# Experts taken in a pattern of ranks by row count, and padding rows left out of the scatter, in a decoder layer with 32 experts

## The chip, the cores and the metric

One core of a Trainium2 chip. The metric is the device time of one execution in microseconds.

## The reference

One layer of a decoder: 512 prompt rows and 8 single-row samples (520 rows of 1024 numbers) go through a combined projection, three mixers (pooling, dilated attention, convolution), an output projection and a layer norm. Then comes the part that matters here, a mixture of experts (fp32 throughout):

```python
logits = xt @ router_w + router_b                 # 520 x 32
top_v, top_i = lax.top_k(logits, 4); gates = softmax(top_v)
hh = xblk @ e_w_in[e] + e_b_in[e]                 # 1024 -> 2048
gate, up = split(hh); gate = min(gate, 7); up = clip(up, -7, 7)
act = gate * sigmoid(1.702 * gate) * (up + 1)
y = act @ e_w_out[e] + e_b_out[e]                 # 1024 -> 1024, weighted by the gate, summed per row
x = layer_norm(alpha * x + moe(x))
```

Each row goes to 4 of the 32 experts, 2080 row visits in all. The weights of one expert are 12 MiB and are used by nobody else.

## The kernel before, in words

`first_block` computes everything up to the router: projection, mixers, first layer norm (`ln1`), router (`route`), and `acc_start`, which writes alpha * x plus the gated output biases to `acc_rows` in DRAM. At its end it counts the rows of each expert. The counts come from five matmuls (L957) into `bS[0]`, and `group_table` (L1219) turns them into groups: each expert's rows are cut into groups of GS = 32, at least one per expert, in the order of the experts. VectorE works out `ends` (the last group of each expert) and, for each group, its expert, its number within the expert, and the ring position. `fields` is turned by TensorE (L964) and `group_rows` packs it into `jobs`. TensorE's bias products of the last two row tiles (`expert_bias`, L924 and L928) stand between the count and that turn. `first_block` ends as a block, and `moe_block` begins on all engines after it.

`moe_block` takes one group after the other. A group is spread over four column groups of the TensorE array, 32 rows in each: `up` multiplies the 32 gathered rows with the eight 1 MiB units of `e_in` (L1473 adds the bias, L1480 multiplies), VectorE and ScalarE make the activation, `down` multiplies with the four 1 MiB units of `e_out` (L1492), ScalarE scales with the gate (L1559). TensorE runs up of group g, then down of group g - 1, then the small matmuls that find the rows of group g + 3 (L1463). GpSimd gathers a group's rows from `x1_rows` (L1412, 128 pieces of 1 KB, with a bounds check that leaves out pads) and adds the result to `acc_rows` by an accumulating indirect DMA (L1419, 128 pieces of 1 KB). A group with fewer than 32 rows is filled with pads; their pieces are added to 32 extra rows of `acc_rows`, from PAD0 on, which are zeroed beforehand.

The weights come through a ring of NSLOT = 18 slots of 1 MiB, so one and a half experts. SyncE issues them in order, expert by expert (L214 by `load`): units 0 to 5 of an expert go into slots that the expert before the last has left (seen by its last group), units 6 to 11 into slots of the expert before it:

```python
was = (j - (NSLOT - UNITS)) % UNITS
if end is not None and was < KT:
    sp.wait_ge(up_done, KT * end + 1 + was)
elif end is not None:
    sp.wait_ge(down_done, NQ * end + 1 + was - KT)
load_unit(sp, unit(slot), e, j, slot)
```

Here `end` is the number of the last group of the expert that used the slot. The loops over groups have room for 96 (MAXG), and groups beyond the last pass as empty turns. When the last scatter has landed, `acc_rows` is read back and the second layer norm makes the output.

Of the kernel before, what the change touches and what calls it, by code (L numbers as in the profile page):

```python
# [29 lines left out]
P = 128  # L30
# [34 lines left out]
NROW = R + GS  # L65


def _columns(widths):
# [10 lines left out]
    ("over", MAXR), ("group", 1), ("third", 10), ("id32", GS)])  # L79
# [22 lines left out]
def constants():  # L102
# [32 lines left out]
    put("third", np.tile(3 * np.arange(1, 11), (P, 1)))  # L135
    put("id32", (p[:, None] % GS == np.arange(GS)) & (p[:, None] < 3 * NE))
# [44 lines left out]
def layer(nc, xT, x_prompt, x_sample, pool_prefix, conv_prefix, state_pool, state_conv, cache_k, cache_v,  # L181
          w_in, pool_w, chan, w_o, ln1_g, ln1_b, router_w, router_b, e_in, e_brow, e_out, e_bout,
          ln2_g, ln2_b, consts, ranks, pbias,
          y_prompt, y_sample, p_pool, p_conv, p_k, p_v, s_pool, s_conv, s_k, s_v):
    x1_dram = nc.dram_tensor("x1_rows", [R, D], F32).ap()
    acc_dram = nc.dram_tensor("acc_rows", [NROW, D], F32).ap()

    with ExitStack() as outer:
        def keep(name, shape, dt=F32):
            return outer.enter_context(nc.sbuf_tensor(name, shape, dt))  # L190

        def sem(name):
            return outer.enter_context(nc.semaphore(name))


        ring = keep("ring", [P, UNITS, 2048])
        cst = keep("cst", [P, NCONST])
        slot_rank = keep("slot_rank", [P, GS * (MAXR + 2)], F16)
        rankm = keep("rankm", [P, NT + 1, NE])
        gates = keep("gates", [P, NT + 1, NE])  # L200
        brow = keep("brow", [P, NQ, 2, QC], BF16)
        jobs = keep("jobs", [1, 3, NGT], I32)
        ends = keep("ends", [1, NE], I32)

        def C(name, rows=P):
            lo, hi = CONST[name]
            return cst[0:rows, lo:hi]

        unit_in = [sem(f"unit_in{u}") for u in range(NSLOT)]

        def load_unit(eng, room, e, j, slot):

            src = e_in[bass.ds(e, 1), j] if j < KT else e_out[bass.ds(e, 1), j - KT]
            eng.dma_start(room, src.rearrange("o p n -> p (o n)")).then_inc(unit_in[slot], 16)  # L214

        first_block(nc, locals())
        moe_block(nc, locals())
# [3 lines left out]
def first_block(nc, o):  # L221
# [3 lines left out]
    ring, rankm, gates, jobs, ends, brow, C, load_unit = (  # L225
        o[k] for k in "ring rankm gates jobs ends brow C load_unit".split())
# [29 lines left out]
    with ExitStack() as ctx:  # L256
# [37 lines left out]
        ssc = sb("ssc", [P, 2, NH * NS])  # L294
# [6 lines left out]
        jf = late[0:1, 2 * D + 14 * NE:2 * D + 14 * NE + 3 * P].rearrange("p (k g) -> p k g", k=3)  # L301
        btok = xtok[:, :, :].rearrange("p u n -> p (u n)")
# [20 lines left out]
        zero = cpre[:, 0:2].rearrange("p i b t -> p (i b t)")[:, 0:D // 4]  # L323
# [19 lines left out]
        zero_made = bsem("zero_made")  # L343
# [31 lines left out]
        pads_zeroed = bsem("pads_zeroed")  # L375
# [15 lines left out]
        brow_ready = bsem("brow_ready")  # L391
        fields_ready = bsem("fields_ready")
# [103 lines left out]
        def _(gp):  # L496
# [50 lines left out]
            nc.gpsimd.memset(zero, 0.0).then_inc(zero_made, 1)  # L547
# [9 lines left out]
        def _(a):  # L557
# [95 lines left out]
            def ln1_root(i):  # L653
# [5 lines left out]
            a.wait_ge(zero_made, 1)  # L659
            a.dma_start(acc_dram[PAD0:PAD0 + GS, :].rearrange("r (c n) -> (r c) n", n=QC), zero  # L660
                        ).then_inc(pads_zeroed, 16)
# [38 lines left out]
            a.wait_ge(pads_zeroed, 16)  # L700
# [4 lines left out]
        def _(pe):  # L705
# [250 lines left out]
            for j in range(NT + 1):  # L956
                mm = nc.tensor.matmul(bS[0][:, (NT + 1) * NE:(NT + 2) * NE], trib[0:rows(j), 1], memb[0:rows(j), j],  # L957
                                      start=j == 0, stop=j == NT)
            mm.then_inc(rank_done, 1)
            for i in (NT - 1, NT):  # L960
                expert_bias(i)
# [7 lines left out]
        def _(d):  # L969
# [249 lines left out]
            def group_table():  # L1219

                COUNT, SUM, SUM2, PASSED, BASE = range(5)
                row = lambda k: tab[:, k]
                ch.do(V.tensor_copy(row(COUNT), bS[0][:, (NT + 1) * NE:(NT + 2) * NE]))
# [14 lines left out]
                ch.do(V.tensor_scalar(fields[:, 1:2], fields[:, 3:4], float(NE - 1), None, ALU.min))  # L1238
                ch.mark(V.tensor_tensor(fields[:, 5:6], C("group"), fields[:, 4:5], ALU.subtract))
                ch.do(V.tensor_scalar(thirds, C("third"), fields[:, 1:2], None, ALU.is_le))  # L1240
                ch.mark(V.tensor_reduce(fields[:, 6:7], thirds, AX.X, ALU.add))
                ch.do(V.tensor_scalar(fields[:, 2:3], fields[:, 5:6], float(MAXR), None, ALU.min))
                V.tensor_tensor(fields[:, 0:1], fields[:, 1:2], fields[:, 6:7], ALU.add).then_inc(fields_ready, 1)
# [33 lines left out]
def moe_block(nc, o):  # L1277

    ring, slot_rank, rankm, gates, brow, jobs, ends, C, sem, load_unit, unit_in = (
        o[k] for k in "ring slot_rank rankm gates brow jobs ends C sem load_unit unit_in".split())  # L1280
# [4 lines left out]
    with ExitStack() as ctx:  # L1285
# [83 lines left out]
        def _(sp):  # L1369
            def end_of(e):  # L1370
                return sp.value_load(ends[0:1, bass.ds(e, 1)], min_val=0, max_val=MAXG - 1)
# [11 lines left out]
            ahead = NSLOT - UNITS  # L1383
            for j in range(ahead):
                load(1, 1, j, None)
            end0 = end_of(0)
            for j in range(ahead, UNITS):
                load(1, 1, j, end0)
            sp.dma_start(l2g[:, :], o["ln2_g"].partition_broadcast(P)).then_inc(ln2_in, 16)
            sp.dma_start(l2b[:, :], o["ln2_b"].partition_broadcast(P)).then_inc(ln2_in, 16)  # L1390
            with sp.Fori(0, (NE - 2) // 3) as three:
                for i in range(3):
                    before, last_but_one = end_of(3 * three + i + 1), end_of(3 * three + i)
                    for j in range(UNITS):
                        load(3 * three + i + 2, (i + 2) % 3, j, last_but_one if j < ahead else before)
# [10 lines left out]
        def _(gp):  # L1406
# [10 lines left out]
            def scatter(c, i):  # L1417
# [3 lines left out]
                    in_=y[:, i], in_offset=None, compute_op=ALU.add).then_inc(scattered, 16)  # L1421
# [344 lines left out]
```

## Time and profile before

| | |
|---|---|
| median of three runs | 1549.1 us (1548.63, 1549.1, 1553.25) |
| the profiled execution | 1553.53 us |
| its span | 1551.6 us |
| mean granted TensorE clock | 0.906 |
| groups, experts | 82, 32 |
| first block | to about 386 us |
| groups, first start to last start | 398.3 to 1487.3 us |
| HBM read | 446.7 MB |

A profile row of the form "L1480 PE MATMUL pu<-ring,xgT" is a group of instructions of one line of the kernel on one engine. A timeline row gives the start in us, the length in us, and after "idle before" how long the engine had been idle and what ended that. The expert part is 70% of the span, so it's read group by group: each group's first matmul has the line L1473.

### The profile page before, as it was taken

The page shows a single profiled execution, that of the slowest core. Times are in us where ns is not written, and L with a number is a line of the kernel's source. Part 1 is how long each engine was busy: PE and PEld are TensorE (multiplying, and loading weights), DVE is VectorE, ACT ScalarE, POOL GpSimd, SP SyncE. Part 2 cuts the span into 40 slices and gives each one's busy share as a digit, 9 for nine tenths or more (in the row PEclk, how much of TensorE's full clock was granted, in tenths as well). Part 3 has the DMA queues.
Part 4 walks back from the last instruction along what each step waited for, and adds up shares of the span by engine and source line. Part 5 has one row for each costly group of instructions (what it writes and reads, how often), then busy time and mean ns, then how long its engine had stood idle before and what let it go on. Part 6 is the DMA issues. An engine that isn't in the chain of part 4 may idle for free.

```text
span 1551.6 us, 35703 instructions
## 1 busy us (share of the span) xinstructions
PE 1305.5 (84%) x12455; PEld 582.6 (38%) x12456; DVE 539.4 (35%) x1798; ACT 151.4 (10%) x330; POOL 298.1 (19%) x247
## 2 busy tenths in 40 slices
PE   5998889997687978999976888999889999989960
PEld 5885333563232323333321332333323333333420
DVE  1994522236331322333321332333223333323325
ACT  0003232021000000000000000000000000000002
POOL 7000231100120211222220221222112222222223
PEclk9999679876797989999986998999999999999985
DMA  9600432116799899999899999949999779999553
GB/s 307 185 3 31 161 97 109 45 55 263 315 408 416 314 416 412 403 368 407 334 412 421 418 412 413 410 150 410 414 414 377 296 259 371 407 412 414 200 175 114
DMA packets 93495, 463.47 MB, mean 299 GB/s; under 512 B 10676, under 2 KB 37265, under 8 KB 43693
## 3 DMA queue, kind: packets, MB, share of 16 engines
q1 hardware_dynamic: 74315, 432.95, 68.8%
q0 software_dynamic: 16640, 22.30, 6.7%
q10 hardware_dynamic: 2514, 7.88, 1.3%
q8 instruction: 15, 0.25, 0.1%
q14 instruction: 11, 0.09, 0.0%
HBM read 446.66 MB, written 19.42 MB: 300 GB/s over the span
## 4 chain that ended last, share of the span: by engine, by line
PE 52%; DMA 15%; issue 5%; DVE 1%; SPq 0%; POOLq 0%; POOL 0%; ACT 0%; ACTq 0%; DVEq 0%
PE pu L1480 32%; PE py L1492 17%; DMA ring<-in_e_in 14%; PE pu L1473 2%; PE raw L1463 1%; DMA xq<-x_rows,idx 0%; DVE bn L1685 0%; DVE ring L1701 0%; DMA ring<-acc_rows 0%; DVE mv L1695 0%; SPq L214 0%; POOLq L1285 0%; POOL ring L1455 0%; POOLq L1437 0%; DVE mv L1687 0%
## 5 line engine op out<-in xcount | busy, mean ns | idle before, releaser
L1480 PE MATMUL pu<-ring,xgT 128*32 128x512 f32 x5248 | 625.6, 623 | 64.4 <-DMA ring<-in_e_in 64.4
L1480 PEld LDWEIGHTS pu<-ring,xgT 128*32 128x32 f32 x5248 | 164.6, 112 | 462.5 <-issue 326.1
L1492 PE MATMUL py<-ring,hid 128*32 128x256 f32 x5248 | 306.5, 386 | 11.6 <-issue 11.6
L1419 POOL DMA_INDIRECT acc_rows<-y,idx x82 | 129.1, 1575 | 865.5 <-ACT y L1559 855.9
L1492 PEld LDWEIGHTS py<-ring,hid 128*32 128x32 f32 x5248 | 177.9, 112 | 165.3 <-issue 74.3
L1656 DVE TENSOR_SCALAR gg<-pu 128x256 f32<-128x256 f32 x82 | 34.8, 425 | 539.3 <-PE pu L1480 539.3
L718 PE MATMUL pair<-xt,ring 128*128 128x260 f32 x448 | 101.5, 390 | 15.8 <-DMA xt<-in_xT 15.8
L1553 ACT ACTIVATE ss<-gg 128x256 f32<-128x256 f32 x82 | 34.3, 418 | 802.2 <-DVE gg L1656 802.2
L1670 DVE STREAM_TRANSPOSE hid<-hq 128x256 f32<-128x256 f32 x82 | 36.5, 445 | 195.6 <-ACT y L1559 195.6
L1412 POOL DMA_INDIRECT xq<-x_rows,idx x85 | 88.8, 1044 | 48.1 <-issue 32.3
L718 PEld LDWEIGHTS pair<-xt,ring 128*128 128x128 f32 x448 | 86.8, 194 | 29.3 <-DMA xt<-in_xT 15.5
L1473 PE MATMUL pu<-brow,chosen 128*32 128x512 bf16 x328 | 33.0, 391 | 75.3 <-issue 72.2
L1597 DVE TENSOR_TENSOR onehot<-rankm,slot_rank 128x160 bf16 (+1 forms) x344 | 88.8, 321 | 1.7
L988 DVE SCALAR_TENSOR_TENSOR conv<-conv,chan_sb 128x512 f32<-128x512 f32 x90 | 70.1, 779 | 3.1
L1559 ACT ACTIVATE y<-py,gate 128x256 f32 x82 | 38.9, 474 | 252.9 <-PE py L1492 252.9
L887 PE MATMUL pair<-ring,mix 128*128 128x512 f32 x128 | 59.9, 630 | 0.3 <-ACT mix L575 0.3
L544 POOL TENSOR_SCALAR ring<-ring,negm 128x128 f32<-128x128 f32 (+3 forms) x24 | 26.2, 1093 | 174.9 <-DVE negm L1143 174.8
L1463 PE MATMUL raw<-pay,onehot 128*128 128x6 bf16 (+1 forms) x425 | 30.6, 170 | 11.6 <-DVE onehot L1597 11.4
L1463 PEld LDWEIGHTS raw<-pay,onehot 128*128 128x128 bf16 (+1 forms) x425 | 21.8, 95 | 48.2 <-issue 40.3
L1473 PEld LDWEIGHTS pu<-brow,chosen 128*32 128x32 bf16 x328 | 8.9, 93 | 81.8 <-issue 79.9
L887 PEld LDWEIGHTS pair<-ring,mix 128*128 128x128 f32 x128 | 25.8, 204 | 32.2 <-issue 32.2
L1620 DVE STREAM_TRANSPOSE xgT<-xq 128x256 f32<-128x256 f32 x83 | 36.5, 440 | 0.7 <-DMA xq<-x_rows,idx 0.7
(229 smaller groups left out, 749.7 us busy)
## 6 DMA issues: line engine op xcount, KB each, us to landing
ring<-in_e_in SPq DMA_DIRECT2D x256, 1024.0 KB, 15.6
ring<-in_e_out SPq DMA_DIRECT2D x128, 1024.0 KB, 16.7
ring<-in_w_in SPq DMA_DIRECT2D x3, 1536.0 KB, 13.1
ring<-in_w_o SPq DMA_DIRECT2D x1, 4096.0 KB, 13.4
ring<-in_w_in SPq DMA_DIRECT2D x6, 512.0 KB, 12.9
xt<-in_xT SPq DMA_DIRECT2D x2, 1040.0 KB, 9.8
xtok<-in_x_prompt POOLq DMA_DIRECT2D x4, 512.0 KB, 3.6
x_rows<-conv ACTq DMA_DIRECT2D x4, 512.0 KB, 8.5
```

Of the source, the lines that this page charges most:

```text
L718: mm = nc.tensor.matmul(b[:, h, 0:HALF], wcols(lo, lo + P)[:, k], xt[:, k, h * HALF:(h + 1) * HALF], start=k == 0, stop=k == KT - 1)
L887: mm = nc.tensor.matmul(b[:, h], mix[:, k, i * P:(i + 1) * P], wo[:, k, h * 512:(h + 1) * 512], start=k == 0, stop=k == KT - 1)
L988: ch.mark(V.scalar_tensor_tensor(cy[:, i, 0:SEQ], u[:, i, t:t + SEQ], taps[:, i, t:t + 1], cy[:, i, 0:SEQ], ALU.mult, ALU.add))
L1412: nc.gpsimd.indirect_dma_start(out=xq[:, b], out_offset=None, in_=x1_quarters, in_offset=bass.IndirectOffsetOnAxis(ap=idx8[:, c:c + 1], ax ...
L1419: nc.gpsimd.indirect_dma_start(out=acc_quarters, out_offset=bass.IndirectOffsetOnAxis(ap=idx8[:, c:c + 1], axis=0), in_=y[:, i], in_offset ...
L1463: mm = nc.tensor.matmul(raw[:, 0:6], onehot[0:rows(i), i].rearrange("p c s -> p (c s)"), pay[0:rows(i), i], start=i == 0, stop=i == NT)
L1473: nc.tensor.matmul(pu[quarter(c)], chosen[:, :], brow[:, c], start=True, stop=False, skip_group_check=True)
L1480: mm = nc.tensor.matmul(pu[quarter(c)], xgT[:, k], w[:, :, c * QC:(c + 1) * QC], start=False, stop=k == KT - 1, skip_group_check=True)
L1492: mm = nc.tensor.matmul(py[quarter(c), 0:QC], hid[:, 2 * q + f], w[:, f, c * QC:(c + 1) * QC], start=q == 0 and f == 0, stop=q == FT // 2 ...
L1559: nc.scalar.activation(y[:, bass.ds(g % 4, 1)].rearrange("p o n -> p (o n)"), py[:, 0:QC], ACT.Copy, scale=gate8[:, bass.ds(g % 8, 1)]).th ...
L1597: ins = V.tensor_tensor(onehot[:, :, c], rankm[:, :, bass.ds(e, 1)].broadcast_to([P, NT + 1, GS]), slot_rank[:, bass.ds(first, GS)].unsque ...
L1620: V.transpose(xgT[:, :, :].rearrange("p k s -> p (k s)"), xq[:, b]).then_inc(turned, 1)
```

## The change

The experts are no longer taken in the order 0, 1, 2, ... Expert 0 stays first. The other 31 are ranked by their number of rows (ties by index), and the constant `ORDER` says which rank stands at which place. `group_table` first makes, on 32 partitions, a key for each expert, counts how many keys are larger (its rank), and marks the place of that rank; a matmul with ones then spreads the counts in the new order and the numbers of the experts over all partitions. This takes five more small matmuls for the counts as a column, a wait on TensorE (`placed_ready`) ahead of the last two `expert_bias`, one matmul, a wait on VectorE (`ordered`), and three further steps in the table. SyncE reads the expert of each place from a new table `order`. The scatter gets a bounds check, so the pads' pieces, whose rows lie beyond the end of `acc_rows`, are left out; the 32 extra rows, the memset of zeros and the store of them go.

```diff
+ORDER = (0, 16, 11, 10, 17, 18, 14, 9, 20, 1, 21, 15, 12, 24, 13, 8, 25, 7, 26, 6, 27, 5, 22, 19, 4, 28, 23, 3, 30, 2, 29, 31)
...
-    acc_dram = nc.dram_tensor("acc_rows", [NROW, D], F32).ap()
+    acc_dram = nc.dram_tensor("acc_rows", [R, D], F32).ap()
...
-            nc.gpsimd.memset(zero, 0.0).then_inc(zero_made, 1)
...
-            a.wait_ge(zero_made, 1)
-            a.dma_start(acc_dram[PAD0:PAD0 + GS, :].rearrange("r (c n) -> (r c) n", n=QC), zero
-                        ).then_inc(pads_zeroed, 16)
...
+            for j in range(NT + 1):
+                mm = nc.tensor.matmul(bS[0][0:NE, (NT + 2) * NE:(NT + 2) * NE + 1], memb[0:rows(j), j],
+                                      trib[0:rows(j), 1, 0:1], start=j == 0, stop=j == NT)
             mm.then_inc(rank_done, 1)
+            pe.wait_ge(placed_ready, 1)
+            nc.tensor.matmul(bS[0][:, (NT + 3) * NE:(NT + 5) * NE], C("ones", NE),
+                             placed.rearrange("p k e -> p (k e)"), start=True, stop=True).then_inc(ordered, 1)
             for i in (NT - 1, NT):
                 expert_bias(i)
...
-                ch.do(V.tensor_copy(row(COUNT), bS[0][:, (NT + 1) * NE:(NT + 2) * NE]))
+                ch.mark(V.scalar_tensor_tensor(key, bS[0][0:NE, (NT + 1) * NE:(NT + 2) * NE], float(NE), C("tie", NE),
+                                               ALU.mult, ALU.add))
+                ch.mark(V.tensor_copy(own[:, 2:3], column))
+                ch.do(V.scalar_tensor_tensor(mine, column, float(NE), C("tie1", NE), ALU.mult, ALU.add))
+                ch.do(V.tensor_scalar(beats, key, mine, None, ALU.is_gt))
+                ch.do(V.tensor_reduce(better, beats, AX.X, ALU.add))
+                ch.mark(V.tensor_scalar(placed[:, 0], C("place", NE), better, own[:, 2:3], ALU.is_equal, ALU.mult))
+                V.tensor_scalar(placed[:, 1], C("place", NE), better, C("group", NE), ALU.is_equal, ALU.mult
+                                ).then_inc(placed_ready, 1)
+                d.wait_ge(ordered, 1)
+                ch.mark(V.tensor_copy(row(EXPERT), bS[0][:, (NT + 4) * NE:(NT + 5) * NE]))
+                ch.do(V.tensor_copy(row(COUNT), bS[0][:, (NT + 3) * NE:(NT + 4) * NE]))
+                ch.mark(V.tensor_copy(order[:, :], tab[0:1, EXPERT]))
...
-                ch.do(V.tensor_scalar(fields[:, 1:2], fields[:, 3:4], float(NE - 1), None, ALU.min))
+                ch.do(V.tensor_scalar(fields[:, 7:8], fields[:, 3:4], float(NE - 1), None, ALU.min))
+                ch.do(V.tensor_scalar(row(HERE), C("exp"), fields[:, 7:8], None, ALU.is_equal))
+                ch.do(V.tensor_tensor(row(HERE), row(HERE), row(EXPERT), ALU.mult))
+                ch.mark(V.tensor_reduce(fields[:, 1:2], row(HERE), AX.X, ALU.add))
...
+            def expert_at(o):
+                return sp.value_load(order[0:1, bass.ds(o, 1)], min_val=0, max_val=NE - 1)
...
                     before, last_but_one = end_of(3 * three + i + 1), end_of(3 * three + i)
+                    e = expert_at(3 * three + i + 2)
                     for j in range(UNITS):
-                        load(3 * three + i + 2, (i + 2) % 3, j, last_but_one if j < ahead else before)
+                        load(e, (i + 2) % 3, j, last_but_one if j < ahead else before)
...
-                    in_=y[:, i], in_offset=None, compute_op=ALU.add).then_inc(scattered, 16)
+                    in_=y[:, i], in_offset=None, compute_op=ALU.add,
+                    bounds_check=NQ * R - 1, oob_is_err=False).then_inc(scattered, 16)
```

## Rows read from the trace of the kernel before

**Rows 1.** The page's fourth part: the chain that ended last, by engine and line.

```profile
PE 52%; DMA 15%; issue 5%; DVE 1%; SPq 0%; POOLq 0%; POOL 0%; ACT 0%; ACTq 0%; DVEq 0%
PE pu L1480 32%; PE py L1492 17%; DMA ring<-in_e_in 14%; PE pu L1473 2%; PE raw L1463 1%; DMA xq<-x_rows,idx 0%; DVE bn L1685 0%; DVE ring L1701 0%; DMA ring<-acc_rows 0%; DVE mv L1695 0%; SPq L214 0%; POOLq L1285 0%; POOL ring L1455 0%; POOLq L1437 0%; DVE mv L1687 0%
```

**Rows 2.** Timeline of TensorE: starts of groups, beside the long intervals.

```profile
437.11 0.40 PE L1473 MATMUL pu<-brow,chosen 128*32 128x512 bf16 x4 [1.05 <-issue]
...
461.29 0.40 PE L1473 MATMUL pu<-brow,chosen 128*32 128x512 bf16 x4 [0.76 <-issue]
...
492.62 0.40 PE L1473 MATMUL pu<-brow,chosen 128*32 128x512 bf16 x4 [0.53 <-issue]
...
516.40 0.40 PE L1473 MATMUL pu<-brow,chosen 128*32 128x512 bf16 x4 [0.76 <-issue]
...
540.90 0.40 PE L1473 MATMUL pu<-brow,chosen 128*32 128x512 bf16 x4 [1.15 <-issue]
...
564.05 0.40 PE L1473 MATMUL pu<-brow,chosen 128*32 128x512 bf16 x4 [1.17 <-issue]
...
575.72 0.40 PE L1473 MATMUL pu<-brow,chosen 128*32 128x512 bf16 x4 [0.54 <-issue]
...
595.76 0.40 PE L1473 MATMUL pu<-brow,chosen 128*32 128x512 bf16 x4 [0.55 <-issue]
...
801.07 0.40 PE L1473 MATMUL pu<-brow,chosen 128*32 128x512 bf16 x4 [0.78 <-issue]
...
834.06 0.40 PE L1473 MATMUL pu<-brow,chosen 128*32 128x512 bf16 x4 [1.14 <-issue]
...
864.78 0.40 PE L1473 MATMUL pu<-brow,chosen 128*32 128x512 bf16 x4 [1.20 <-issue]
...
1487.34 0.40 PE L1473 MATMUL pu<-brow,chosen 128*32 128x512 bf16 x4 [1.04 <-issue]
```

**Rows 3.** Groups of instructions between 437 and 1487 us, the costliest first.

```profile
L1480 PE MATMUL pu<-ring,xgT 128*32 128x512 f32 x4992 | 593.2, 621 | 64.4 <-DMA ring<-in_e_in 64.4
...
L1419 POOL DMA_INDIRECT acc_rows<-y,idx x78 | 122.8, 1574 | 824.6 <-ACT y L1559 815.0 <-issue 9.7
L1412 POOL DMA_INDIRECT xq<-x_rows,idx x78 | 81.5, 1045 | 25.1 <-issue 25.1
```

**Rows 4.** Windows: length, busy time (and count) of each engine, PEclk, DMA, GB/s.

```profile
437.00:1487.00 1050.00, 916.80 (x10686) 353.27 (x10686) 309.76 (x1249) 69.61 (x156) 204.24 (x156) 0.95 0.94 372
...
461.00:493.00 32.00, 19.54 (x145) 4.39 (x149) 4.26 (x17) 0.93 (x3) 2.62 (x2) 0.68 1.02 419
...
865.00:938.00 73.00, 66.89 (x822) 27.13 (x818) 23.17 (x92) 5.36 (x12) 15.65 (x12) 1.00 1.03 411
960.00:1091.00 131.00, 122.02 (x1502) 50.05 (x1502) 43.54 (x176) 9.34 (x21) 28.80 (x22) 1.00 0.85 333
```

**Rows 5.** SyncE's queue: an issue in the timeline, and its waits (us, times, longest).

```profile
517.98 1.19 SPq L214 DMA_DIRECT2D ring<-in_e_in  x2
...
SPq L214 <- PE pu L1480: 385.0, 152, 37.3
SPq L214 <- PE py L1492: 383.6, 120, 13.9
```

**Rows 6.** The page's third part: the queue of GpSimd's DMAs, packets, MB, share.

```profile
q0 software_dynamic: 16640, 22.30, 6.7%
```

**Rows 7.** Timeline at the end of the first block.

```profile
374.09 0.39 PE L924 MATMUL bS<-cst,gates 128*32 128x128 f32 x1
...
374.48 0.32 DVE L1268 TENSOR_TENSOR rankm<-rankm,bS 128x160 f32<-128x160 f32 x1
...
379.06 3.56 PE L928 MATMUL pair<-conv,up 32*8 32x512 f32 x4 [0.37 <-ACT up L670]
...
379.66 0.16 DVE L1243 TENSOR_TENSOR xt<-xt 128x1 f32<-128x1 f32 x1
...
382.56 1.44 PE L964 MATMUL bT<-cst,xt 128*1 128x128 f32 x6
...
386.26 3.00 SPq L214 DMA_DIRECT2D ring<-in_e_in  x6
```

**Rows 8.** Timeline of TensorE: the down product of the last group.

```profile
1510.02 5.05 PE L1492 MATMUL py<-ring,hid 128*32 128x256 f32 x64 [11.56 <-issue]
```

## What was predicted

> **What bounds the kernel now.** The profiled execution took 1553.53 us, its span is 1551.6; the three timed runs have a median of 1549.1, which is 4.4 below it. I read the page's chain first: it lies on TensorE for 52% and on one load, `ring<-in_e_in`, for 14% [rows 1]. So the expert part alternates between two limits, and the average says nothing; the group starts must be read one by one.
>
> Line 1473 is the first matmul of each group of 32 rows, so its rows are the clock of the expert part [rows 2]. From the fourth group (437.11) to the last (1487.34) there are 78 intervals in 1050.2 us. 68 of them lie between 11.6 and 12.4 us and average 12.0: this is TensorE's own time for a group. Ten are longer; the rows shown bound five of them: 31.3, 23.2, 20.0, 33.0 and 30.7 us. Together the ten exceed 12.0 by 1050.2 - 78 x 12.0 = 114 us. The trace names what ended that idle time: the expert weights, with 64.4 us of it before line 1480 and the rest in matmuls that trickle behind the loads at a granted clock of 0.68 in one such stretch [rows 3, 4].
>
> The DMA side is just as uneven. In stretches with long intervals the core moves 410 to 420 GB/s with the DMA engines busy all the time; from 960 to 1091 it moves only 333 [rows 4]. There the loads wait for room: SP waited 385 us for up-matmuls and 384 us for down-matmuls to free slots [rows 5]. So each resource waits for the other in turn. What ends last at a long interval is the load of the expert that is just starting.
>
> **An account of the lead.** The reference's inputs send 38, 59, 15, 99, 14, 41, 79, 83, 93, 52, 106, 48, 10, 27, 96, 37, 35, 74, 137, 38, 54, 36, 87, 71, 148, 82, 64, 75, 34, 91, 135 and 22 rows to experts 0 to 31. Rounded up to groups of 32: 2 2 1 4 1 2 3 3 3 2 4 2 1 1 3 2 2 3 5 2 2 2 3 3 5 3 2 3 2 3 5 1, together 82, as many as the trace has scatters (78 of them from the fourth group on [rows 3]).
> The load of one expert is 12 x 1.0486 = 12.58 MB; with it go 2.56 groups' gather (25.4 real rows of 4 KB, 0.104 MB) and scatter (32 rows, 0.131 MB), 0.60 MB. At 415 GB/s, the middle of the busy stretches [rows 4], that is 31.8 us. TensorE takes 12, 24, 36, 48, 60 us for 1 to 5 groups. So a place with 1 group costs 19.8 us of lead, one with 2 costs 7.8, and 3, 4, 5 groups give back 4.2, 16.2, 28.2.
> The lead has a cap, since the ring holds 18 units, one and a half experts: the seventh unit of the next expert goes into a slot that the last group of the present one must first read. Such a group starts at 516.40 and SP issues at 517.98 [rows 2, 5], only one group ahead of the need. The size of the cap I take from the intervals: expert 3 has 4 groups (lead full), then experts 4 and 5 cost 19.8 + 7.8 = 27.6, and TensorE lost 11.1 + 8.0 = 19.1, so the cap was 8.5; after expert 10, experts 11 to 13 cost 47.4 and 20.9 + 18.7 = 39.6 was lost: 7.8.
> With lead = min(cap, lead + gain - cost) from expert 1 on, and every amount below zero a stall, a cap of 7.5 gives for the old order 19.8 (expert 2), 12.3, 7.8 (4, 5), 19.8, 19.8 (12, 13), 3.6, 7.8 (15, 16), 7.8, 7.8 (20, 21), 3.6 (28) and five times 0.3: 111.6 us against 114 in the trace. Caps of 6.4 and 8.4 give 118.2 and 106.8, so 7.5 is what I keep.
>
> **The change, part by part.**
> 1. The order. Expert 0 stays first, the others are ranked by rows, and the pattern gives the groups 2 2 3 3 2 2 3 3 2 5 2 3 3 2 3 3 2 3 2 3 1 4 2 2 4 1 2 5 1 5 1 1. The same account: 7.8 (place 5), 3.6 (18), 15.6 (20), 7.8 (23), 12.3 and 7.8 (25, 26), 12.3 (28), 12.3 (30) and seven times 0.3: 81.6 us. The last one delays the last group, which waits for its own weights. Gain: 111.6 - 81.6 = 30.0 us. With the rate at 31.4 or 32.2 us per expert both sums move together (gain 29.7, 30.0); with caps of 6.4 and 8.4 it is 25.6 and 31.8. The average group time doesn't change, as three code positions still take turns. Of the 1-group experts only one still follows another, at the very end, where the second has nothing after it.
> 2. The pads. 82 x 32 - 2080 = 544 of 2624 scattered rows are pads, 20.7%. The software queue took 6.7% of the span of all DMA engines, 104 us, for 16640 packets [rows 6]; the scatters are 10.7 of its 22.3 MB and, at 1 KB each, 10496 of its packets, so 50 to 66 us, or 0.6 to 0.8 us each. If a pad costs nothing any more, 0.13 to 0.17 us per group goes, 0.3 to 0.4 per expert; by bytes at 415 GB/s it is 0.17 per expert. This counts only while the loads set the pace, which in the new order is in some 13 experts: 2 to 5.5 us. I take 3. The ends are 0, if a skipped piece costs as much as a written one, and 13.6, if all of it lay on the path. POOL's own instruction (1574 ns for a scatter, 1045 for the bounds-checked gather [rows 3]) may grow; POOL has 815 us of idle time before it.
> 3. The setup. Before, TensorE goes from the count matmuls straight to the bias of the last two tiles, and that pair ends the block: 374.09, then 379.06, then the turn of the fields at 382.56, while VectorE's table was ready at 379.8 [rows 7]. Now TensorE first does five small matmuls (0.4 us), waits for five chained VectorE steps of 0.2 us on 32 columns (behind the two on `rankm`, which end at 374.8), and does one more matmul: it reaches the bias some 2.8 us later. Queued behind this wait are both bias products, and with them VectorE's two `acc_start`, the fields and the block's end at 386.26. VectorE's own chain grows by 2.4 before and 0.7 us after the table, which ends at 382.9, still ahead of TensorE. I take +2.8, from 0 (were the bias not on the path) to +5 (with semaphore delays). The start of the experts' loads moves with it.
> 4. The memset of the zeros and its store had no one behind them: nothing. SP's third register load per expert stands at an expert's first unit, where SP waits for a slot anyway: nothing; were SP not waiting it would be under 1 us per expert. The tail after the last group (idle loop passes to 1510.02 [rows 8]) stays, and its 11.6 us hide the last landing.
> Sum: -30.0 - 3 + 2.8 = -30.2 us. On the profiled execution that is 1553.5 - 30.2 = 1523.3; on the median 1549.1 - 30.2 = 1518.9.
>
> **Where a rule of the skill speaks against it.** In the stretch 461 to 493 the core moved 419 GB/s [rows 4]. The Trainium skill, "DMA: Bandwidth & Descriptors", section "Where 436 GB/s comes from", says that for loads from HBM the HBM share of a core, about 358 GB/s, binds. By that an expert's 12.58 MB would take an estimated 35 us, and order could do little. The trace doesn't agree: 419 was measured. The first rival below has the same mechanism, worked out from rows.
>
> **Rivals.**
> - The loads bind nearly throughout. They are slower than TensorE's mean of 30.8 us even at 31.8, but the lead of 7.5 rescues part. Were the mean rate of the whole part, 372 GB/s [rows 4], all that the loads can have, 13.18 MB would take 35.4 us, and the account gives 178 us before and 168 after: gain 10, time 1549.1 - 10 - 3 + 2.8 = 1539. Against it: that would have shown as 178 us of stalls, and there are 114. Nearly the same time comes out if the lead doesn't refill in the pairs of 3 groups that the pattern relies on (4.2 each). Chance 0.12 for a gain of 5 to 20.
> - The pads weigh more, since the DMA queues of weights and scatters interfere: near 13 us instead of 3, time 1509. For it: the busy stretches. Against it: a third of the loads wait for room. Chance 0.08.
> - Slower: a skipped piece costs more than a written one. 2176 pieces over 16 DMA engines are 136 each; to turn the forecast to +5 us they'd have to cost 35 us, 0.26 us each, over twice what a whole 1 KB piece took (50 to 66 us over 656 pieces per engine, 0.08 to 0.10 us), and that on the path throughout. At 0.3 us: 1524 + 38 x 0.8 = about 1554. For it: an accumulating scatter with pieces skipped is nowhere in the trace. Against it: the gathers skip pads already. Chance 0.04.
> - The change doesn't do what it says: ranks by wrong counts, for instance an order that puts single groups side by side. The account with every lead lost gives 165 us for any order. Within 0.3% of before; chance 0.02.
> The Trainium skill, same page, section "Specifications", says that below 512 B a DMA engine reads, modifies and writes; if skipped pieces turned into such small writes, this would be the third rival. No row here shows it for a scatter.
>
> **How the numbers follow.** Forecast 1519, chance 0.74, for gains of 20 to 40 us. 0.3% is 4.6 us, about what a measurement can tell from none. Range 1508 to 1534: below it the pads' upper end with the larger cap, above it most of the rival of slow loads, the smaller cap and the setup's upper end. Faster 0.94, same 0.02, slower 0.04.
>
> **What the changed profile would show.** Line 1473 with long intervals at places 5/6, 20/21, 23/24, 25 to 27, 28/29 and 30/31 and none above 2 us elsewhere; their excess near 80 us; first group at about 401; line 1480 waiting 45 to 50 us for weights; 2176 fewer KB written by the software queue. The forecast is wrong if the single groups' intervals exceed 28 us, if the stretches without long intervals also lose time, or if the first group starts beyond 404.

## The result, and the profile after

The changed kernel takes 1535.99 us (median of four runs, 1533.34 to 1537.62), the kernel before, run beside it, 1550.44. The ratio is 0.9901, 95% interval 0.9889 to 0.9914: some 15 us faster where 30 were forecast, and just beyond the upper end of the range. The profiled execution took 1537.62 us with a span of 1535.8.

The page of the changed kernel (line, engine, out<-in xcount | busy us, mean ns | idle before), beside [rows 1, 3, 6]:

```profile
PE 55%; DMA 11%; issue 6%; DVE 1%; SPq 0%; POOLq 0%; POOL 0%; ACT 0%; ACTq 0%; DVEq 0%
...
L1511 PE MATMUL pu<-ring,xgT 128*32 128x512 f32 x5248 | 613.1, 614 | 45.1 <-DMA ring<-in_e_in 45.1
L1449 POOL DMA_INDIRECT acc_rows<-y,idx x82 | 129.1, 1575 | 842.3 <-ACT y L1590 832.2
...
q0 software_dynamic: 16640, 20.04, 5.8%
q8 instruction: 15, 0.25, 0.1%
```

L1511 is what L1480 was, L1504 what L1473 was, L1523 what L1492 was. The chain spends less on the load (11% of the span where it was 15%), and the matmuls wait less for weights: in the 78 group intervals from the fourth start on, their line waited 64.4 us before the change [rows 3] and now waits 37.3. The software queue moves 2.26 MB less in as many packets as before; GpSimd's own instruction is unchanged (1575 ns against 1574). So the order and the pads do what the diff says.

Windows over the same 78 intervals, and groups of instructions in them:

```profile
446.00:1457.00 1011.00, 897.55 (x10690) 354.71 (x10690) 310.10 (x1251) 69.45 (x156) 204.26 (x156) 0.97 0.94 376
```

```profile
L1511 PE MATMUL pu<-ring,xgT 128*32 128x512 f32 x4992 | 575.6, 608 | 37.3 <-DMA ring<-in_e_in 37.3
...
L1449 POOL DMA_INDIRECT acc_rows<-y,idx x78 | 122.8, 1574 | 786.9 <-ACT y L1590 776.8 <-issue 10.1
```

The granted clock rose from 0.95 to 0.97 and the rate from 372 to 376 GB/s [rows 4].

TensorE's timeline of the changed kernel, starts of groups beside some of the long intervals [rows 2], and the last group's down product [rows 8]:

```profile
446.16 0.40 PE L1504 MATMUL pu<-brow,chosen 128*32 128x512 bf16 x4 [1.09 <-issue]
...
579.63 0.40 PE L1504 MATMUL pu<-brow,chosen 128*32 128x512 bf16 x4 [0.52 <-issue]
598.55 0.40 PE L1504 MATMUL pu<-brow,chosen 128*32 128x512 bf16 x4 [0.53 <-issue]
...
1078.28 0.40 PE L1504 MATMUL pu<-brow,chosen 128*32 128x512 bf16 x4 [0.95 <-issue]
1102.47 0.40 PE L1504 MATMUL pu<-brow,chosen 128*32 128x512 bf16 x4 [0.54 <-issue]
...
1372.47 0.40 PE L1504 MATMUL pu<-brow,chosen 128*32 128x512 bf16 x4 [1.38 <-issue]
1396.88 0.40 PE L1504 MATMUL pu<-brow,chosen 128*32 128x512 bf16 x4 [1.25 <-issue]
...
1456.75 0.40 PE L1504 MATMUL pu<-brow,chosen 128*32 128x512 bf16 x4 [0.79 <-issue]
...
1492.65 1.94 PE L1523 MATMUL py<-ring,hid 128*32 128x256 f32 x16 [11.71 <-issue]
```

Only seven intervals are long now. Their excess over 12.0 us, beside the forecast for the place whose shortness causes each: 6.9 (forecast 7.8, place 5), 5.7 (3.6, place 18), 12.2 (15.6, 20), 8.2 (7.8, 23), 11.1 (12.3, 25), 7.9 (7.8, 26) and 12.4 (12.3, 28), and from the last group's start to its down product 35.9 us instead of 22.7, 13.2 more (12.3, place 30). Below, the pace is the mean of the intervals that are not long, and the second interval is the one from the second group's start to the third's.

The whole budget, from group starts read off both timelines:

| stretch | before | after | difference |
|---|---|---|---|
| to the first group's start | 398.30 | 400.81 | +2.5 |
| first three intervals | 38.81 | 45.35 | +6.5 |
| next 78: waits for weights (excess of the long ones) | 113.4 | 64.5 | -48.9 |
| next 78: pace (the other intervals against 12.0; means 12.01 and 12.14) | 0.8 | 10.1 | +9.2 |
| last group's start to the end | 64.3 | 79.0 | +14.8 |
| sum, with 78 x 12.0 = 936.0 on both sides (the pieces are rounded) | 1551.6 | 1535.8 | -15.8 |

Two of the five were not in the forecast at all: 6.5 us in the first three intervals and 9.2 us in the pace. The experiments are mainly about these.

TensorE in the second interval, first before, then after:

```profile
416.94 3.64 PE L1492 MATMUL py<-ring,hid 128*32 128x256 f32 x64
420.81 0.36 PE L1463 MATMUL raw<-pay,onehot 128*128 128x6 bf16 x5 [0.23 <-issue]
423.24 0.40 PE L1473 MATMUL pu<-brow,chosen 128*32 128x512 bf16 x4 [2.07 <-issue]
```

```profile
419.36 3.64 PE L1523 MATMUL py<-ring,hid 128*32 128x256 f32 x64
423.39 0.23 PE L1494 MATMUL raw<-pay,onehot 128*128 128x6 bf16 x3 [0.39 <-issue]
429.07 0.28 PE L1494 MATMUL raw<-pay,onehot 128*128 128x6 bf16 x2 [5.45 <-issue]
431.55 0.62 PE L1504 MATMUL pu<-brow,chosen 128*32 128x512 bf16 x4 [2.20 <-issue]
```

TensorE stops for 5.45 us between two matmuls of one unbroken run, waiting for nothing that the profile shows. I take q8 for the queue of TensorE's code: its transfers shift in time when TensorE's code is padded, and the kernels below with 114 instructions or more added have 16 of them instead of 15. It has one transfer while TensorE stands (DMA view from 426 to 428: packets, MB, share; in narrower windows it lies between 426.5 and 426.75, and the stop ends at 429.07):

```profile
q8 instruction: 1, 0.02, 3.4%
```

In all 1011 us from 446 to 1457 it has none; the queues in that stretch are

```profile
q1 hardware_dynamic: 49943, 363.67, 86.8%
q0 software_dynamic: 14976, 16.30, 7.4%
q14 instruction: 2, 0.02, 0.0%
```

The last q8 transfer before that stretch comes at 432.8, and the next one after it at about 1495. So TensorE reads code from memory in its first passes through the loop and not again until the last group.

The pace, by the first matmul of a group (line 1473 before, 1504 after) over the 78 intervals: idle time before it in us, times. This view adds the weight loads' idle time to that of the matmuls, so the one pause of a group is counted twice:

```profile
L1473 PE MATMUL pu<-brow,chosen x312: 381/389/390, 437.1 to 1475.1; 128*32 128x512 bf16 x156
...
  issue: 144.4, 156
```

```profile
L1504 PE MATMUL pu<-brow,chosen x316: 381/389/391, 446.2 to 1456.8; 128*32 128x512 bf16 x158
...
  issue: 159.1, 158
```

For the matmuls alone, over the same 78 groups, it is 69.1 us before and 75.6 after: 0.89 us per group before, 0.97 after. Set group by group against the kernel of experiment 3 that has the old pace (68.3 us), an ordinary group of the changed kernel mostly lies within 0.05 us of it up to its last matmul on L1494; then the turn to the next group (the branches and the register load at the loop's end and head) takes 0 to 0.24 us longer, 0.10 on average.

### The profile page after: what moved, and what is told of

It reads as the page before. It is cut to its first block, busy times and chain, and to the rows that moved or that the text cites. A ratio compares the mean times of both kernels' runs of the same rounds, so it can differ in the third digit from the quotient of the medians.

```text
span 1535.8 us, 35947 instructions
## 1 busy us (share of the span) xinstructions
PE 1294.0 (84%) x12462; PEld 584.3 (38%) x12463; DVE 541.4 (35%) x1810; ACT 151.2 (10%) x330; POOL 298.0 (19%) x246
## 3 DMA queue, kind: packets, MB, share of 16 engines
q0 software_dynamic: 16640, 20.04, 5.8%
## 4 chain that ended last, share of the span: by engine, by line
PE 55%; DMA 11%; issue 6%; DVE 1%; SPq 0%; POOLq 0%; POOL 0%; ACT 0%; ACTq 0%; DVEq 0%
PE pu L1511 34%; PE py L1523 18%; DMA ring<-in_e_in 10%; PE pu L1504 2%; PE raw L1494 1%; DMA xq<-x_rows,idx 0%; DVE bn L1716 0%; DMA ring<-acc_rows 0%; DVE ring L1732 0%; DVE mv L1726 0%; SPq L219 0%; POOLq L1310 0%; POOL ring L1486 0%; POOLq L1468 0%; DVE mv L1718 0%
## 5 line engine op out<-in xcount | busy, mean ns | idle before, releaser
L1511 PE MATMUL pu<-ring,xgT 128*32 128x512 f32 x5248 | 613.1, 614 | 45.1 <-DMA ring<-in_e_in 45.1
L1511 PEld LDWEIGHTS pu<-ring,xgT 128*32 128x32 f32 x5248 | 165.0, 111 | 433.7 <-issue 334.4
L1523 PE MATMUL py<-ring,hid 128*32 128x256 f32 x5248 | 305.0, 385 | 12.4 <-issue 12.4
L1449 POOL DMA_INDIRECT acc_rows<-y,idx x82 | 129.1, 1575 | 842.3 <-ACT y L1590 832.2
L1523 PEld LDWEIGHTS py<-ring,hid 128*32 128x32 f32 x5248 | 178.5, 112 | 162.5 <-issue 71.6
L720 PE MATMUL pair<-xt,ring 128*128 128x260 f32 x448 | 101.3, 389 | 15.1 <-DMA xt<-in_xT 15.1
L1504 PE MATMUL pu<-brow,chosen 128*32 128x512 bf16 x328 | 33.2, 394 | 82.2 <-issue 78.6
L720 PEld LDWEIGHTS pair<-xt,ring 128*128 128x128 f32 x448 | 86.8, 194 | 28.5 <-DMA xt<-in_xT 14.8
L1494 PE MATMUL raw<-pay,onehot 128*128 128x6 bf16 (+1 forms) x425 | 30.8, 170 | 17.2 <-DVE onehot L1628 11.3
L1504 PEld LDWEIGHTS pu<-brow,chosen 128*32 128x32 bf16 x328 | 8.9, 93 | 88.8 <-issue 86.3
L1494 PEld LDWEIGHTS raw<-pay,onehot 128*128 128x128 bf16 (+1 forms) x425 | 21.8, 95 | 54.0 <-issue 46.1
## 6 DMA issues: line engine op xcount, KB each, us to landing
ring<-in_w_o SPq DMA_DIRECT2D x1, 4096.0 KB, 13.2
```

The lines of the kernel that those rows point to most:

```text
L720: mm = nc.tensor.matmul(b[:, h, 0:HALF], wcols(lo, lo + P)[:, k], xt[:, k, h * HALF:(h + 1) * HALF], start=k == 0, stop=k == KT - 1)
L1449: nc.gpsimd.indirect_dma_start(out=acc_quarters, out_offset=bass.IndirectOffsetOnAxis(ap=idx8[:, c:c + 1], axis=0), in_=y[:, i], in_offset ...
L1494: mm = nc.tensor.matmul(raw[:, 0:6], onehot[0:rows(i), i].rearrange("p c s -> p (c s)"), pay[0:rows(i), i], start=i == 0, stop=i == NT)
L1504: nc.tensor.matmul(pu[quarter(c)], chosen[:, :], brow[:, c], start=True, stop=False, skip_group_check=True)
L1511: mm = nc.tensor.matmul(pu[quarter(c)], xgT[:, k], w[:, :, c * QC:(c + 1) * QC], start=False, stop=k == KT - 1, skip_group_check=True)
L1523: mm = nc.tensor.matmul(py[quarter(c), 0:QC], hid[:, 2 * q + f], w[:, f, c * QC:(c + 1) * QC], start=q == 0 and f == 0, stop=q == FT // 2 ...
```

## Experiments

Theory: the change puts 14 TensorE instructions ahead of the expert loop (five bf16 matmuls and an fp32 one that runs twice, each with its weight load). The loop's code therefore lies 14 instructions further on against the blocks in which it is fetched (q8 moves 0.25 MB in 15 transfers, so some 16 KB each; that a block holds 256 instructions is put to the test), and both losses come from that. Rival: they come from the data or the schedule, such as the new order, the skipped pieces or the later start.

**1. Move the code, nothing else.** In three kernels, waits that are met at once stand ahead of TensorE's first product; two of these calls make one instruction (the profiles count 242, 14 and 2 instructions more).

```diff
+            for _ in range(484):                  # 242 instructions; 28 and 4 calls in the other two
+                pe.wait_ge(ld["xt"], 0)
             pe.wait_ge(ld["xt"], 32)
```

Changed kernel with 242, so that the shift against before is 256:

> The changed kernel with 242 more instructions (waits that are met at once) at the head of TensorE's stream, where it idles 15.8 us for its first data. With the change's own 14 added instructions that is 256, so the expert loop's code stands where it stood before, modulo 256 instructions. Theory 'code position' (the change moved TensorE's code by 14 instructions, which lengthened each group by 0.13 us and put a stop of 5.5 us into the second group): about 1520 us, ordinary groups again 12.0 us on average, group 2 to 3 again 13.5 instead of 19.4 us. Rival 'data side' (the added register loads, the bounds check or the new table slow the groups): 1536 us, 12.14 us a group, 19.4 us.

Kernel before with 14:

> The kernel before with 14 such instructions at the head of TensorE's stream and nothing else. Theory 'code position': the whole penalty appears without the change: about 1549 + 16 = 1565 us, 12.14 us a group, 19.4 us from group 2 to 3. Rival 'data side': 1549 us, 12.0 us a group.

Changed kernel with 2:

> The changed kernel with 2 such instructions, so that the shift against before is 16. If what counts is the place within a short line of 4 instructions, the ordinary group is back at 12.0 us (10 us less in all, about 1526), while the stop in the second group may stay or move. If what counts is the place within a block of 256, nothing or little changes: 12.14 us, 1536. Rival 'data side': 1536.

Measured: 1534.63 us (1532.85 to 1535.6), 1559.04 (1556.97 to 1561.76) and 1534.97 (1533.53 to 1537.92), the kernel before beside them 1552.13. In the profile the 242 give a pace of 12.03 us and a second interval of 13.96, close to the 12.01 and 13.50 of before. The 14 alone give the kernel before a pace of 12.12 and a second interval of 19.40, with a stop of 5.38 us:

```profile
418.88 0.23 PE L1465 MATMUL raw<-pay,onehot 128*128 128x6 bf16 x3 [0.49 <-issue]
424.49 0.28 PE L1465 MATMUL raw<-pay,onehot 128*128 128x6 bf16 x2 [5.38 <-issue]
```

It is the same place, after the same third matmul, with the old order and the old pads. So the rival falls, and b_nop14 prices the shift by itself: ratio 1.0044 (1.0027 to 1.0062), 7 us. That is less than half of the 16 that were expected. Both losses are there (5.9 us in the first three intervals, 7.1 in the pace), but the first group starts 1.7 us earlier and the long intervals' excess falls from 113.4 to 107.3. The 242 mend both losses but gave back nearly all of it at the start, so the expected 1520 us were missed: they took all of the 27.21 us ahead of the first product, 0.11 us each, where TensorE had been idle for 15.1 us; of these 12 us, 7.9 were left at the first group (408.72 against 400.81). The 2 change nothing in the time or the pace (12.14); the stop comes one matmul, so two instructions, earlier: after the second raw matmul, 4.98 us.

**2. The order alone.** The changed kernel with the experts in the order of their numbers:

```diff
-ORDER = (0, 16, 11, 10, 17, 18, 14, 9, 20, 1, 21, 15, 12, 24, 13, 8, 25, 7, 26, 6, 27, 5, 22, 19, 4, 28, 23, 3, 30, 2, 29, 31)
+ORDER = tuple(range(32))
...
-    tie = np.where(np.arange(NE) == 0, 1e6, -np.arange(NE))
+    tie = -8192.0 * np.arange(NE)
```

> The changed kernel with the same code but constants that make the order 0, 1, 2, ... again (rank by index). Theory of the lead account: long intervals together about 110 us (114 less the pads' 3) instead of 77 with the last group's own stall, so 1536 + 33 = 1569 us. Rival 'the order is worth less than the account says and the pads did the rest': below 1555.

Measured: 1564.26 us (1563.09 to 1565.18), 29.3 more than the changed kernel with 2 waits on the same chip; 1569 was expected. The order is worth what the account gave it (30.0), at nearly the same position of the code (shift 14 against 16). Pace 12.12 and second interval 19.25 stay as in the changed kernel: neither is a matter of the order.

**3. Move the code at no cost.** The waits now stand in a branch that is never taken, so they only take room (7 more instructions make the loop and the jump):

```diff
+            with pe.Fori(0, 2) as never:
+                with pe.If(never == 5):
+                    for _ in range(470):          # shift 256; 86 calls: shift 64; 342: shift 192
+                        pe.wait_ge(ld["xt"], 0)
             pe.wait_ge(ld["xt"], 32)
```

> The changed kernel with a block of 235 waits that is jumped over and never executed, at the head of TensorE's first stage, where it waits for its first operands anyway (with the jump and its loop 242 instructions; together with the 14 that the change added, 256, so that the expert loop's code lies again where the kernel before had it against blocks of 256). Theory of the code's position: the 12 us that the executed waits cost at the start are gone, the interval between groups is 12.03 us and the second interval 13.9, so 1526 to 1528 us, ratio 0.983 to 0.985. If what the 242 executed waits mended was something that their execution did (a later start, a fuller queue), the pace stays at 12.14 and the time at 1535 us.

Half a block, as 114 executed waits (228 calls in the form of experiment 1), which fit into TensorE's idle start:

> The changed kernel with 114 instructions of TensorE more ahead of the first product (waits that are met at once), 128 with those that the change added: half a block of 256. At 0.11 us each they take 12.5 us of the 15.1 us for which TensorE waits there for its first operands, so they cost nothing at the start. If any shift away from a multiple of 256 costs the same, the pace stays at 12.14 us and the time at 1535 us; if the cost hangs on which of the loop's blocks is cut where, the pace is another one between 12.0 and 12.3 us, worth 78 times the difference: 1525 to 1548 us. If the executed waits as such mend the pace, 1526 us.

> The changed kernel with a jumped-over block of 50 instructions, jump and loop counted: shift 64 against the kernel before. The runs so far show a pace of 12.01 us at shifts 0 and 256, 12.03 at 128, and 12.12 to 12.15 at 14 and 16; the second interval 13.5 to 14.5 us at 0 and 256 and 19.4 to 20.1 at 14, 16 and 128. If the cost of the turn hangs on one narrow stretch of positions, the pace here is 12.01 to 12.04 and the time 1526 to 1534 us, by the second interval; if it hangs on how far the loop's head stands behind the block's edge, it is 12.1 or more and the time 1535 us or more.

> The changed kernel with a jumped-over block of 178 instructions, jump and loop counted: shift 192. By the narrow stretch: pace 12.01 to 12.04 and 1524 to 1534 us, by the second interval; otherwise a pace of 12.1 or more and 1535 us or more.

| shift (instructions) | kernel | pace | second interval | time, median | ratio to before, 95% |
|---|---|---|---|---|---|
| 14 | the change | 12.14 | 20.33 | 1537.09 | 0.9894 (0.9878 to 0.9911) |
| 64 | jumped over | 12.01 | 20.07 | 1532.64 | 0.9864 (0.9847 to 0.9882) |
| 128 | executed | 12.03 | 19.96 | 1534.01 | 0.9877 (0.9861 to 0.9894) |
| 192 | jumped over | 12.06 | 19.86 | 1530.55 | 0.9864 (0.9847 to 0.9880) |
| 256 | jumped over | 12.02 | 14.54 | 1524.15 | 0.9826 (0.9806 to 0.9846) |

The row of shift 14 is a second set of the changed kernel, on the chip of shifts 64 and 192; 128 and 256 ran on another one, so the ratios are what to compare:

> The changed kernel as it stands, so that the kernels beside it are compared with it on one chip: 1535 to 1537 us.

The block at shift 256 brings the change to 1524 us. By the ratios that is 10.5 to 11.6 us faster than the changed kernel in its two sets, by the medians 12 to 13; nothing that TensorE executes in the loop differs. The two profiled executions differ by 12.3 us: 5.9 in the first three intervals, 3.5 from the fourth start to the last, 2.8 in the last group. The windows from 422 to 434 us, first the changed kernel, then this one (columns as in [rows 4]):

```profile
422.00:434.00 12.00, 3.96 (x41) 1.36 (x37) 2.17 (x10) 0.47 (x1) 2.86 (x2) 0.68 1.01 391
```

```profile
422.00:434.00 12.00, 8.66 (x83) 2.66 (x78) 2.17 (x10) 0.47 (x1) 2.85 (x2) 0.86 1.02 402
```

The stop costs twice: where TensorE stands, the granted clock is lower too (0.68 in this stretch against 0.86), and the up product after the stop takes 9.38 us against 8.41. TensorE's pause before the first matmul of a group is back at the old value, 142.9 us, again with the weight loads counted in:

```profile
L1508 PE MATMUL pu<-brow,chosen x312: 381/389/390, 440.2 to 1435.4; 128*32 128x512 bf16 x156
...
  issue: 142.9, 156
```

And the place where TensorE first stops moves through the code as the code moves. TensorE's timeline at shifts 64, 128 and 192 (L1527, L1525 and L1527 are the down product, L1498 and L1496 the raw matmuls):

```profile
420.00 2.78 PE L1527 MATMUL py<-ring,hid 128*32 128x256 f32 x48
423.92 1.07 PE L1527 MATMUL py<-ring,hid 128*32 128x256 f32 x16 [1.15 <-issue]
430.40 0.38 PE L1498 MATMUL raw<-pay,onehot 128*128 128x6 bf16 x5 [5.40 <-issue]
```

```profile
419.95 1.05 PE L1525 MATMUL py<-ring,hid 128*32 128x256 f32 x16
423.98 4.30 PE L1525 MATMUL py<-ring,hid 128*32 128x256 f32 x48 [2.98 <-issue]
...
430.26 0.36 PE L1496 MATMUL raw<-pay,onehot 128*128 128x6 bf16 x5 [1.98 <-issue]
```

```profile
421.82 6.37 PE L1527 MATMUL py<-ring,hid 128*32 128x256 f32 x64 [4.58 <-issue]
```

At shift 14 the long stop comes after all 64 down products and three raw matmuls; at 64 the first break is after 48 down products, at 128 after 16, at 192 before the first. Each matmul is two instructions with its weight load: from shift 64 to 128 the code moved by 64 instructions, and the first break by 32 matmuls, which is 64 too. So the first break sits at a fixed place of the code's storage.

The whole of the lost time doesn't sit at one place: at 64 the first break is only 1.15 us, and 5.40 follow ahead of the raw matmuls; at 128 it is 2.98 and then 1.98. Between this down product and the raw matmuls the kernel's text has two more copies of the down product (one per ring position), some 256 instructions that are jumped over. My reading is that the first break is the end of one block and the second the end of the next, passed by that jump. In each of the four kernels the break (at 64 and 128 each of the two) ends 2 to 3.5 us after a q8 transfer. At shifts 0 and 256 the block's end would lie 14 instructions behind the place of shift 14, past the last raw matmul, and no long stop is seen in this pass. No run tests this reading by itself.

The pace follows another rule: it is bad at 14 and 16, a little off at 192 and good at 0, 64, 128 and 256. At shift 64 the expectation of the narrow stretch was met in full (12.01 us, 1532.64 within 1526 to 1534); at 192 the time was (1530.55) and the pace just missed (12.06 against 12.04). At 128 the time is the one expected for an unmended pace (1535), but the pace is mended: the second interval makes the time.

**4. The pads.** The changed kernel, and the one at shift 256, with the pads' rows scattered again (to 32 rows that nobody reads and that aren't zeroed):

```diff
-    acc_dram = nc.dram_tensor("acc_rows", [R, D], F32).ap()
+    acc_dram = nc.dram_tensor("acc_rows", [R + GS, D], F32).ap()
...
-                    in_=y[:, i], in_offset=None, compute_op=ALU.add,
-                    bounds_check=NQ * R - 1, oob_is_err=False).then_inc(scattered, 16)
+                    in_=y[:, i], in_offset=None, compute_op=ALU.add).then_inc(scattered, 16)
```

> The changed kernel with the pads scattered again: the scatter has no bound, and its pad rows, 2176 pieces of 1 KB, go to 32 extra rows behind the sums, which nothing reads (so only the price of moving them is left). By the sum's term: 3 us slower than with the pads skipped (0 to 5.5), 1536 to 1541 us, the row of the software queue back at 22.3 us. By the rival in which pads weigh more: 13 us slower, 1549 us. By the rival in which a skipped piece costs as much as a written one: no difference, 1535 us, though the queue's row falls.

> The kernel with the jumped-over block, with the pads scattered again to 32 extra rows. The same edit cost the changed kernel about 1 us (1537.0 against 1536.0, on another chip), less than the sum's 3 us. With the code's position mended TensorE has 10 us less of pauses, so more of the waits for weights is bare and the transfers weigh more: if the pads' 2.2 MB and 0.3 us per group count there, 3 us or more over the kernel with the block (1527 us or more); if the scatters lie in time that the weight loads don't need, 1524 to 1525 us.

Measured: 1537.01 us, ratio 0.9904 (0.9889 to 0.9919), against 0.9894 and 0.9901 for the changed kernel in its two sets, each uncertain by 0.0015 too; and 1530.55 us, ratio 0.9855 (0.9838 to 0.9871), against 0.9826 at shift 256. The page again shows as many packets with the bytes back:

```profile
q0 software_dynamic: 16640, 22.25, 6.6%
```

So skipping the pads is worth 0 to 2 us in the changed kernel and 4.5 (0 to 9) in the one at shift 256, where the long intervals' excess rises from 70.0 to 73.0 us with them. That rise proves little: two profiled executions of the changed kernel itself have 64.5 and 67.3, and with its pads back the changed kernel has 63.4. The 3 us of the sum lie between; 13 don't fit either pair. The pairs weren't run on one chip in one set, so a difference of 3 us between them is not settled.

**5. Another order by the same account**, on top of shift 256:

> The kernel with the jumped-over block and, beside it, another order of ranks, found by searching with the account of loads and groups that the prediction used: (0, 17, 3, 24, 4, 22, 1, 18, 11, 28, 15, 26, 2, 30, 10, 8, 16, 13, 23, 9, 21, 5, 29, 7, 14, 19, 12, 25, 20, 6, 27, 31). The account gives this order 3 us less waiting for weights than the order of the change, so 1523 to 1525 us if the account holds to a few us; if it doesn't (another spread of the waits over the run, so another load rate in them), 1527 us or more.

Measured: 1520.88 us (1520.01 to 1522.97), ratio 0.9797 (0.9784 to 0.9811): 3.3 us under the same kernel with the change's order, on the same chip and in the same set, about as the account gave (3); by the ratios it is 4.5, with an interval of about 1 to 8. Worked again with the prediction's own numbers (31.8, 7.5, 12.0) the account gives 79.8 us of waiting for this order and 81.6 for the change's. The two profiles have 80.2 and 81.9 (the long intervals' excess, and what the last group's stretch has over the 64.3 of before). It is the fastest kernel of this study, 15 us under the change.

## Why the prediction was wrong

- **The order, term 1 (-30.0): right.** Measured alone it is 29.3 us. All eight stalls came at the places that the account listed, with sizes 0.1 to 3.4 us from its own.
- **"The average group time doesn't change, as three code positions still take turns": this step failed.** Position in the ring was thought of, position in instruction storage was not. The shift by 14 instructions costs the ordinary group 0.13 us, 9 us in all (0.10 and 7 in the kernel before), and the second interval some 5 to 6 us. Of the pace only a part reaches the end: at shift 256 the pace gains 9.0 us over the changed kernel between the fourth and the last start, but the excess of the long intervals grows from 64.5 to 70.0, so 3.5 are left. That is the account at work, since a slower group gives the loads more lead: with 12.14 instead of 12.0 us a group the account itself gives 77.0 instead of 81.6. The stop in the first pass has no such cover: ratio 0.9864 at shift 64, where only the pace is mended, against 0.9826 where both are, so some 6 us.
- **The setup, term 3 (+2.8): right.** The first group starts 2.5 us later, SyncE's first load 2.9 us (389.18 against 386.26 [rows 7]). The timeline shows TensorE reaching the last bias product 2.0 us later, 381.03 against 379.06:

```profile
375.44 0.69 PE L966 MATMUL bS<-xt,cst 32*128 32x64 f32 x2 [1.91 <-DVE xt L1240]
...
381.03 3.57 PE L930 MATMUL pair<-conv,up 32*8 32x512 f32 x4 [0.37 <-ACT up L673]
...
389.18 2.63 SPq L219 DMA_DIRECT2D ring<-in_e_in  x5
```

- **The pads, term 2 (-3): not refuted**, 0 to 2 us in one pair and 4.5 in the other.
- **SyncE, GpSimd, the memset, term 4 (nothing): nothing seen.** SyncE waits for its slots as before; between the fourth and the last start the two sums are 726 us after and 732 before (over the whole of before 769 [rows 5]):

```profile
SPq L219 <- PE pu L1511: 368.8, 153, 38.6
SPq L219 <- PE py L1523: 357.0, 116, 14.6
```

- **The sum.** With the position put back, the gain over the kernel before on the same chip is 27.8 us by the medians and 27 by the ratio (24 to 30), against 30.2 forecast. So 11 to 12 of the missing 15 us are the code's position, and some 3 us, with as much doubt, the error of all other terms together.
- **The rivals.** That the loads bind nearly throughout gave 1539, close to the measured time, and would have been right by accident: its sign would be stalls of 168 us, and the trace has 64.5 and the last group's 13. The result alone would have confirmed the wrong mechanism. No rival had the position of the code; the prediction's own condition, that the stretches without long intervals lose time, is what met it.

The Trainium skill, "Runtime: NRT & Kernel Launch", section "Instruction fetch mechanics", says that code is refilled in blocks of 16 KB, 256 instructions, and that the cost of crossing from one to the next is "mostly hidden". The trace agrees with the size (15 transfers, 0.25 MB) and not with the cost in the loop's first pass: TensorE stood for 5.45 us. It also says that a taken branch to code outside a window of two blocks forces a fetch before work goes on. The 5.40 us ahead of the raw matmuls at shift 64, behind the jump over two copies of the down product and with a q8 transfer in them, agree with that. No run here shows it for the loop's turn: q8 carries nothing from 446 to 1457 us, and yet the turn costs 0.10 us more at one position than at another.

**What stays open.** Why the turn of a loop whose code is not fetched again hangs on its position, and why it is slow at shifts 14 and 16 and not at 64. The traces show the longer pause and no cause for it. Open too is whether two block ends are what splits the loss of the first pass at shifts 64 and 128.

## What to carry to other kernels

Read where the lead of a two-sided pipeline (loads against compute) is earned and spent, place by place: that account gave the stalls, their sizes and the value of a second order to a few us. But before crediting an edit in one part, count what it does to the code of the busiest engine: a handful of instructions ahead of a hot loop moves the loop against its fetch blocks. Where the ordinary iteration has changed though nothing in it was edited, pad with instructions that are jumped over, and look at the first pass of the loop for a stop with a code transfer in it.

## What the hardware showed that was not expected

- A pass of the loop took 0.13 us more on average (12.14 against 12.01), 0.10 of it at the turn, with the same instructions, no code fetched, and the code 14 instructions further on. In the kernel before, the same shift made it 0.10 (12.12).
- In the loop's first pass TensorE lost 4.6 to 6.6 us in one or two stops, each ending 2 to 3.5 us after a transfer on the code's queue; the first of them moved by 64 instructions when the code did. At shift 256 a pause of 1.25 us is left ahead of the raw matmuls, against 0.23 in the kernel before.
- An instruction made of two waits that are already met took TensorE 0.11 us (242 of them, 27.2 us).
- Pieces skipped by the bound of an accumulating scatter leave the number of packets (16640) and GpSimd's instruction (1575 ns) as they were; only their bytes go.
